# Two tiles of each output norm scaled on GpSimd, and three exchanges of order in the scan

## What is computed

```python
def rms_norm(x, g):
    y = xf * lax.rsqrt(jnp.mean(xf * xf, axis=-1, keepdims=True) + RMS_EPS)
    return (y * g.astype(jnp.float32)).astype(x.dtype)
...
        h = h + rms_norm(mix, g_post_mix[layer])       # first output norm
        ffn = conv_gated_mlp(rms_norm(h, g_pre_ffn[layer]), ...)
        h = h + rms_norm(ffn, g_post_ffn[layer])       # second output norm
...
    decay_ij = jnp.exp(jnp.where(causal, seg, -jnp.inf))
    y_diag = jnp.einsum('bcgeij,bcjgep->bcigep', cb[:, :, :, None] * decay_ij, xdt)   # SSD
    y_a = rms_norm_2(y_a * jax.nn.silu(z_a), ssd_norm_w)
    o_b = rms_norm_2(o_b, gla_norm_w).reshape(bsz, L, GLA_VALUE_WIDTH) * jax.nn.silu(g_b)   # GLA
```

## Time and profile before

| | us |
|---|---|
| median of 3 runs | 840.57 |
| the profiled execution | 840.04 |
| its span in the trace | 838.2 |
| TensorE busy | 828.9 |
| VectorE busy | 623.1 |
| ScalarE busy | 505.2 |
| GpSimd busy | 124.2 |

### The profile page before, as it was taken

The page is one execution under the profiler, slowest core; times in us unless marked ns, Lnnn a source line. Parts: engine busy times, 40 slices in busy tenths (PEclk is TensorE's granted clock), DMA queues, the critical chain, the costliest instruction groups (busy, mean ns, idle before and its releaser), DMA issues.

```text
span 838.2 us, 16865 instructions
## 1 busy us (share of the span) xinstructions
PE 828.9 (99%) x6768; PEld 799.4 (95%) x6768; DVE 623.1 (74%) x1055; ACT 505.2 (60%) x877; POOL 124.2 (15%) x119
## 2 busy tenths in 40 slices
PE   9999999999999999999999999999999999999997
PEld 8999999999999999999999999999999999888896
DVE  6657888886666689777664478999889696568765
ACT  7447566555444576555554368787978554356755
POOL 1000000000000305433441100043515010000002
PEclk9999999999999999999999999999999999999999
DMA  9754334445555536655665535645555376654331
GB/s 320 264 159 143 134 114 164 127 146 180 178 184 192 170 101 202 206 178 184 194 193 187 195 90 164 193 139 181 162 162 175 102 231 187 187 173 129 127 101 51
DMA packets 39854, 139.81 MB, mean 167 GB/s; under 512 B 4433, under 2 KB 5089, under 8 KB 39649
## 3 DMA queue, kind: packets, MB, share of 16 engines
q1 hardware_dynamic: 38160, 135.90, 50.9%
q10 hardware_dynamic: 1616, 2.84, 1.1%
HBM read 137.65 MB, written 1.06 MB: 165 GB/s over the span
## 4 chain that ended last, share of the span: by engine, by line
PE 88%; DVE 6%; ACT 3%; issue 1%; POOL 1%; DMA 0%; DVEq 0%; SPq 0%; ACTq 0%; POOLq 0%
PE ps L1806 66%; PE ps L1871 4%; PE ps L1809 4%; PE ps L1830 4%; DVE weights_lo L1076 2%; PE ps L2006 1%; PE ps L1991 1%; PE ps L2020 1%; PE ps L2275 1%; PE ps L2293 1%; DVE arena L1386 1%; PE ps L1927 1%; ACT weights_hi L543 1%; PE ps L2283 1%; PE ps L2135 1%
## 5 line engine op out<-in xcount | busy, mean ns | idle before, releaser
L1076 DVE TENSOR_TENSOR weights_lo<-raw_weights,weights_hi 128x1024 fp32r<-128x1024 f32 x251 | 312.3, 1248 | 83.2 <-ACT weights_hi L543 82.0
L543 ACT ACTIVATE weights_hi<-raw_weights 128x1024 fp32r<-128x1024 f32 x250 | 262.2, 1053 | 145.5 <-PE ps L1806 61.1
L1806 PE MATMUL ps<-x_hi,weights_hi 128*128 128x256 f32 (+3 forms) x1184 | 341.8, 289 | 0.3 <-DVE weights_lo L1076 0.2
L1806 PE MATMUL ps<-x_lo,weights_hi 128*128 128x256 f32 (+3 forms) x1184 | 333.7, 282 | 0.0
L1806 PE MATMUL ps<-x_hi,weights_lo 128*128 128x256 f32 (+3 forms) x1184 | 333.0, 281 | 0.0
L1806 PEld LDWEIGHTS ps<-x_hi,weights_hi 128*128 128x128 f32 x1184 | 222.8, 188 | 6.8 <-issue 5.6
L1806 PEld LDWEIGHTS ps<-x_lo,weights_hi 128*128 128x128 f32 x1184 | 222.9, 188 | 0.6 <-issue 0.4
L1806 PEld LDWEIGHTS ps<-x_hi,weights_lo 128*128 128x128 f32 x1184 | 223.2, 189 | 0.0
L1806 PE MATMUL ps<-y_hi,weights_hi 128*128 128x256 f32 (+1 forms) x488 | 137.7, 282 | 0.0
L1806 PE MATMUL ps<-y_lo,weights_hi 128*128 128x256 f32 (+1 forms) x488 | 137.4, 282 | 0.0
L1806 PE MATMUL ps<-y_hi,weights_lo 128*128 128x256 f32 (+1 forms) x488 | 137.1, 281 | 0.0
(11 more groups left out here) (280 smaller groups left out, 1185.9 us busy)
## 6 DMA issues: line engine op xcount, KB each, us to landing
raw_weights<-weights_in SPq DMA_DIRECT2D x251, 512.0 KB, 4.0
arena<-decay_rows ACTq DMA_DIRECT2D x8, 256.0 KB, 4.0
masks<-masks_in SPq DMA_DIRECT2D x1, 1186.0 KB, 8.4
raw_weights<-weights_in SPq DMA_DIRECT2D x4, 256.0 KB, 4.4
hidden<-xT_in SPq DMA_DIRECT2D x3, 272.0 KB, 5.0
hidden<-xT_in SPq DMA_DIRECT2D x1, 276.0 KB, 3.1
gate_w<-gate_w_in ACTq DMA_DIRECT2D x1, 256.0 KB, 3.7
out<-arena ACTq DMA_DIRECT2D x1, 256.0 KB, 2.1
```

The costliest lines, as they stand in the source:

```text
L543: a.sig(A(whi[:, s * CW:(s + 1) * CW], raw[:, (c % RAW) * CW:(c % RAW + 1) * CW], ACT.Copy), "hi_ready")
L1076: d.sig(TT(wlo[:, s * CW:(s + 1) * CW], raw[:, (c % RAW) * CW:(c % RAW + 1) * CW], whi[:, s * CW:(s + 1) * CW].bitcast(F32), ALU.subtract) ...
L1806: ins = mm(bank(BANK_OF[no])[:, 0:b - a], wt, x_[:, kt, a:b], start=s0, stop=s1)
```

## The change

At the output norms two tiles (`FAR = (2, 4)`, the third and the fifth) leave VectorE's `normed`. GpSimd multiplies them by the channel's gain between two additions of squares, before the inverse root is known, and by the inverse root afterwards (`far_normed`), as soon as both halves of `rpost` are there. VectorE's `add` of these tiles waits for GpSimd. In the scan three pieces change places: on GpSimd, at p = 1, `ssd_add(1)` goes behind `ssd_weights(3)`; on ScalarE, at p = 2 and 3, `gla_rms(p - 1)` goes ahead of `take_values(p)`; on VectorE, at p = 2 and 3, `gla_norm(p - 1)` goes ahead of `z_half` of `ez u`.

```diff
+        FAR = (2, 4)
...
-            def add_squares(base, t0, count=KT - 1):
+            def add_squares(base, t0, count=KT - 1, gain_post=None):
                 for i in range(1, count):
                     pool.wait_ge(S("sq_ready"), base + i + 1)
+                    if gain_post is not None and i in FAR:
+                        m = mout[:, i, t0:T]
+                        g.step(nc.gpsimd.tensor_scalar(m, m, pcol(gain_post, i), None, ALU.mult))
                     g.settle()
...
+            def far_normed(nth, t0):
+
+                pool.wait_ge(S("rms_half"), nth // 2)
+                pool.wait_ge(S("rms_ready"), nth)
+                g.settle()
+                for kt in FAR:
+                    m = mout[:, kt, t0:T]
+                    g.sig(nc.gpsimd.tensor_tensor(m, m, rpost[:, t0:T], ALU.mult), "far_normed")
+
-            add_squares(KT, TA)
+            add_squares(KT, TA, gain_post="g_post_mix")
+            far_normed(2, TA)
...
-            add_squares(3 * KT, META)
+            add_squares(3 * KT, META, gain_post="g_post_ffn")
+            far_normed(4, META)
...
                 gla_products(p)
-                ssd_add(2 * p - 1)
+                if p > 1:
+                    ssd_add(2 * p - 1)
                 ssd_weights(2 * p + 1)
+                if p == 1:
+                    ssd_add(1)
                 ssd_add(2 * p)
...
                     feed(("ev", p))
+                    gla_rms(p - 1)
                     take_values(p)
-                    gla_rms(p - 1)
                     feed(("ez", u))
...
-                    dve.wait_ge(S("normed"), first + kt + 1)
+                    if kt in FAR:
+                        dve.wait_ge(S("far_normed"), (nth // 2 - 1) * len(FAR) + FAR.index(kt) + 1)
+                    else:
+                        dve.wait_ge(S("normed"), first + kt + 1 - sum(f < kt for f in FAR))
...
-                    if kt + 1 < KT:
+                    if kt + 1 < KT and kt + 1 not in FAR:
                         normed(kt + 1)
...
                     feed(("ev", p))
+                    gla_norm(p - 1)
                     z_half(("ez", u), zs[:, 0, :])
-                    gla_norm(p - 1)
                     feed(("ez", u))
```

## The result

The changed kernel takes 841.99 us (median of 14 runs, 841.56 to 844.16), the kernel before 840.3 (14 runs, 839.9 to 841.61): a ratio of 1.0021, 95% interval 1.0014 to 1.0028, or +1.7 us. The forecast was +1.45, counted from the 840.57 of the first three runs, so 842.0.

What follows compares the result with a forecast made beforehand. TensorE, busy 828.9 of 838.2 us, was taken as the bound, at norms paced by VectorE. Terms 0.65 + 0 + 0.8 + 0 = +1.45 gave 842.0 us against 840.57; own range 841.0 to 843.0, 8-in-10 range 839.6 to 843.5.

Steps and rivals of the forecast that it cites:

- the norms: Output norms: GpSimd's turns cost VectorE more than the removed products save; +0.33 each, +0.65 together.
- GpSimd's exchange: Scan, p = 1: TensorE's 1.5 wait goes, but VectorE is 0.9 later and delays `gla_kv`; +0.8.
- the exchanges at p = 2 and 3: Scan, ScalarE and VectorE reordered: taken as 0, with ends -0.7 and +0.9.
- One sign: Norms: the first of GpSimd's two final multiplications would take 1.2 to 1.5.
- The lower bound, -1.3: Both norms: if GpSimd's operations cost VectorE nothing, TensorE saves 0.5 at each and another 0.3 at 504.76.
- The multiplications by the gain: GpSimd, early at the norms: priced like an addition, 0.75 alone or 1.50 taking turns; 0, bounds 0 to +0.5.
- the cover: First norm: 1.1 between GpSimd's last addition of squares and TensorE's need; its end moves 0.3 to 0.6, inside it.
- the sum 0.85 + 0.95 + 0.6 = 2.4: Scan, p = 1: what GpSimd's three operations cost VectorE after the exchange, against 1.5 before.
- the tanh waits: Rival, p = 2 and 3: `z_half` comes behind the tanh's turn, adding 1.0 to the forecast; 843.0, chance 0.17.
- The port is no matter: Rival, norms and p = 1: GpSimd slips into VectorE's pauses, norms -1.3, exchange -1.5; 837.8, chance 0.10.
- All cancels: Rival: the scan's chain moves less than one chunk split's turn, -0.6, and pays for the norms; 840.6, chance 0.18.
- The exchange only moves TensorE's wait: Scan, p = 1: TensorE's wait only moves from 571 to 583; part of the forecast, without its own chance.

Runs made afterwards that it cites:

- e5: Kernel before, with VectorE's products of the third and fifth tile left out at the norms and nobody making them up: 839.37 us, ratio 0.9987.
- e1: Kernel before with only the output norms changed, the scan as before: 840.83 us, ratio 1.0007.
- e6: Kernel before, plus two idle GpSimd products on a spare buffer at each norm, VectorE's stream untouched: 841.97 us, ratio 1.0020.
- e2: Kernel before with only GpSimd's exchange at p = 1: 841.29 us, ratio 1.0014.
- e8: Kernel before with the exchanges of ScalarE and VectorE at p = 3 alone: 840.5 us, ratio 1.0003.
- e7: Kernel before with the exchanges of ScalarE and VectorE at p = 2 alone: 840.8 us, ratio 1.0002.
- e4: Kernel before with all three exchanges in the scan, the norms as before: 841.55 us, ratio 1.0015.
- e11: Norms changed, scan as before, GpSimd's products by the inverse root held back until VectorE has done tile 0: 841.99 us, ratio 1.0020 to the kernel before.
- e12: e11 with two superfluous GpSimd waits on the inverse root taken out: 841.06 us, ratio 1.0006 to the kernel before.

## Why the prediction was right, and where it was lucky

**The whole.** +1.45 was forecast; the trace has +1.57, the medians +1.7. The bounds 839.6 and 843.5 hold the time, the forecast's own 841.0 to 843.0 too. But the terms did not come out so well: the norms are 0.50 for 0.65, GpSimd's exchange 0.56 for 0.80, the exchanges at p = 2 and 3 0.54 for 0. That -0.15, -0.24 and +0.54 nearly cancel is luck.

**The norms, +0.33 each.** Measured 0.30 and 0.20. Each step is there: 0.45 at the first addition (0.41), 0.55 at the product of tile 1 (0.46), 0.3 and 0.4 won back (0.27 and 0.40), TensorE's first wait near 0.8 (0.77), no wait for the far tiles. VectorE leaves both norms 0.2 late, where I had 0.3, and the matmul at 504.76 comes 0.21 late (505.93, less the 0.96 that was there before). One sign didn't come: I expected 1.2 to 1.5 for the first of GpSimd's two final multiplications, and each takes 0.77 to 0.85. The lower bound, -1.3, is close to the -1.25 of e5, but not as I had added it up. It has 0.3 for a wait until 504.76, where the earlier trace rows show a wait of 0.17, and e5's second norm is only 0.07 better than its first.

**The multiplications by the gain, 0.** Right, as e1 is the sum of e5 and e6. But their price was not: I bounded it by an addition, 0.75 to 1.50. The timeline of GpSimd has 1.38 for one at the second norm, which starts while VectorE splits a chunk, and 1.66 at the first:

```profile
467.03 1.38 POOL L445 TENSOR_SCALAR arena<-arena,params 128x256 f32<-128x256 f32 x1 [5.79 <-ACT arena L715]
...
466.39 1.22 DVE L1095 TENSOR_TENSOR weights_lo<-raw_weights,weights_hi 128x1024 fp32r<-128x1024 f32 x1
467.91 1.23 DVE L1095 TENSOR_TENSOR weights_lo<-raw_weights,weights_hi 128x1024 fp32r<-128x1024 f32 x1 [0.30 <-ACT weights_hi L562]
...
290.83 1.66 POOL L445 TENSOR_SCALAR arena<-arena,params 128x258 f32<-128x258 f32 x1 [0.41 <-ACT arena L715]
292.58 2.97 POOL L447 TENSOR_TENSOR arena<-arena 128x258 f32<-128x258 f32 x3
```

So 1.38 is 0.58 of waiting for the split (it ends at 467.61) and 0.80 of work. At the first norm, where the cover was 1.1, one takes 1.66, over my upper end, for the same reason; the last addition ends at 295.55, 0.16 later than before once the 0.66 of the start is off (294.73 + 0.66 = 295.39). The cover held because GpSimd stood between the additions anyway.

**GpSimd's exchange, +0.8.** The course was right as far as `gla_kv`: the pair of heads at 0.88, VectorE 0.9 late (573.90 - 571.92 - 1.11 = 0.87 at the next halved gate), the wait of 1 to 2 us (1.33 + 0.18; it stands at the turning of x just ahead of `gla_kv`, which also needs VectorE, and at `gla_kv`). The size was not: 0.56, and 0.59 alone. The step that failed is the sum 0.85 + 0.95 + 0.6 = 2.4 for three turns. The rows give (2.32 - 0.76) + (1.76 - 1.22) = 2.10, as the two GLA products lose 1.56 and not 1.8. Less the 1.5 of before that is 0.6, and it stayed 0.6 to the end. Nor did it go on as I wrote, to the pairs of heads at 608 and 641: TensorE took 0.28 of it at `gla_kv` and the other 0.28 at a chunk split at 592.81, and in e2 the two pairs add nothing.

**The exchanges at p = 2 and 3, 0.** Here it failed: +0.54 in the changed kernel. The rival "the tanh waits" took place, with 0.78 and 0.30 us, at about half the price I gave it. The step that failed is that I worked out each place from the times of before, and took a lag at p = 2 for nothing. For p = 3 alone it was off by one term. VectorE there in e8:

```profile
634.56 0.86 DVE L1498 SCALAR_TENSOR_TENSOR arena<-ps,params,arena 128x256 f32<-128x256 f32 x2
635.46 1.76 DVE L1504 TENSOR_TENSOR arena<-arena 128x256 f32<-128x256 f32 x2
637.33 0.42 DVE L1453 SCALAR_TENSOR_TENSOR arena<-ps,rinv 128x256 f32<-128x256 f32 x1
```

The GLA scaling starts at 634.56, 0.2 late from the start included, where I had 634.42. But the two products take 1.76 where I had put 1.3, and the halved gate ends at 637.55 (with the 0.2 taken off), not at 637.0: more than the 0.4 that I had given the rival as its condition. The loss is 0.15. At p = 2 I wrote "0.2 to 0.6 behind" and counted it nothing, as TensorE's pair had 0.7 to win there. TensorE did win 0.46, only 0.16 of it at that pair. What I left out is that the lag doesn't end with p = 2: ScalarE and VectorE take it to p = 3, where TensorE hangs on ScalarE's decays, gives up the 0.46 and is 0.54 late (e7 shows it with p = 3 untouched).

**The other rivals.** "The port is no matter" is out by e6. "All cancels" is out by the time, +1.7 us, where the interval leaves no change out. "The exchange only moves TensorE's wait" is what p = 1 shows, with 0.56 on top.

## What to carry to other kernels

Two engines that share a port don't add up: what an idle-looking engine takes over must be priced by what it does to the busy one, and a test with work that nobody uses, beside one with the work left out, gives both halves of that price in two runs. A wait that is removed from the fastest engine is worth something only if the engines that feed it move too; where they are the bound, follow their lag, not the fast engine's gain, to the next place where it waits for them. When edits of tenths of a us are at stake, compare the same instruction in two traces, place by place, and take off what the start already differs by.

## What the runs showed of the hardware beyond that

**A clock that falls behind the new wait.** In e4, TensorE stood 1.38 us for VectorE at p = 1 and 1.6 us after that wait ran with half the clock. Busy time by stretch (columns as in the earlier trace rows; the granted clock is the third number from the end), first e4, then e2, which had a wait of 1.4 at the same place:

```profile
583.00:585.00 2.00, 1.36 (x17) 0.99 (x18) 1.83 (x4) 2.00 (x4) 1.85 (x2) 1.00 0.82 313
585.00:588.00 3.00, 3.00 (x17) 3.00 (x16) 2.79 (x7) 0.38 (x1) 0.00 (x0) 0.52 0.32 87
```

```profile
585.00:588.00 3.00, 3.00 (x28) 3.00 (x28) 2.79 (x7) 0.22 (x1) 0.00 (x0) 1.00 0.39 93
```

From 585 to 588 the granted clock is 0.52, the lower of its two levels (1.2 GHz) nearly throughout, and 17 matmuls are done where e2 does 28. TensorE is 1.2 us further behind at 594 than in e2 (1.80 against 0.59). About 0.9 of this is made good, since VectorE and ScalarE set the pace there: the steps at p = 2 and p = 3 are -1.00 and +0.67, where the changed kernel has -0.46 and +1.00. The traces of e2 and of the changed kernel don't have the fall, though they have the wait. The timed runs bear out that the two go together: with GpSimd's exchange (the changed kernel, e2, e4) 14 of 36 have a mean granted clock of 0.997 or less, without it 11 of 218. In the changed kernel the five such runs have a median of 842.61, the other nine 841.81, which is +1.5 and nearer to the trace's +1.57 than the +1.7 of all. So a wait of this length can be followed by a fall and need not be; what decides it was not tried.

**GpSimd's stall** of 0.45 us in place of 0.14, there in e11 and gone in e12 with four instructions less in its stream; it costs 1.2 where it loses a turn. Its cause is open.

**GpSimd's multiplication by one value per channel** reads as 1.38 to 1.92 us for 256 or 258 columns in the four traces that have it, but all 16 start during one of VectorE's chunk splits and end 0.80 to 0.82 after it. An addition or multiplication of two tiles of 256 or 258 columns that starts during a split ends 0.58 to 0.63 after it, in all 14 traces. So the multiplication is the longer one by 0.2, not by the factor of nearly two that 1.38 against 0.75 suggests. And it doesn't take a turn from VectorE: the 12 chunk splits that start while it runs keep their 1.21 to 1.23 us, like the one at 467.91 above, where a split that starts during a GpSimd operation with two such tiles takes up to 1.77 (1.76 at 571.23). That is why the multiplications by the gain cost nothing.
